# Two transformer blocks on one core: weight products in halves, with attention steps between them

## The chip, the core and the metric

One core of a Trainium2 chip. A core has engines that each run their own instruction stream in order: TensorE (PE, matrix products; its weight load is PEld), VectorE (DVE), ScalarE (ACT), GpSimd (POOL) and SyncE (SP, which here starts the loads). They meet only through semaphores. PSUM has eight banks of 128 x 512 fp32, in which PE leaves its sums. The metric is the device time of one execution in microseconds.

## The reference

256 tokens of width 1024 go through two blocks, all in fp32. Cut to what matters here:

```python
# first block (h: 256 x 1024)
p  = rmsnorm(h) @ w_in               # q, k, v of three branches, 3 x 1024 gates
o_a = stick_breaking(q_a, k_a, v_a)  # 4 heads of 64
o_b = softmax attention over the 64 keys that an index score picks (top-k)
o_c = gates_c[0]*compressed + gates_c[1]*selected + gates_c[2]*window attention
      # compressed keys: gelu(blocks(15 x 2048) @ w1(2048 x 128)) @ w2
merged = sum_j sigmoid(g_j) * (o_j @ w_up[j])        # j = a, b, c; w_up[j]: 256 x 1024
h += merged @ w_out
h += softmax((rmsnorm(h) @ w_q) @ k_mem.T) @ v_mem @ w_o   # 4 heads, 256 memory rows
h += (silu(a) * b) @ w_ffn_out;  a, b = rmsnorm(h) @ w_ffn_in
x = rmsnorm(h)
# second block; shift, scale, gate = (silu(c) @ w_ada + b_ada) in six parts
y = rms(x) * (1 + scale_m) + shift_m
proj = y @ w_in_2                     # fox q, k, v, gate (8 heads), ret q, k, v, gate (4 heads)
x += gate_m * (concat(rms(fox) * ..., rms(retention) * ...) @ w_out_2)
x += gate_f * (relu(y2 @ w_mlp_in)**2 @ w_mlp_out);  y2 = rms(x) * (1 + scale_f) + shift_f
```

## The kernel before

**Weight blocks.** Every large product is made of weight blocks of 1 MB. SP loads a block into a ring of four (`raw`), ACT rounds it to fp32r (`hi`, L1330), DVE subtracts to get the remainder (`lo`, L1649, the *residue*), into rings of three. PE multiplies three times, hi·hi, hi·lo and lo·hi: 48 matmuls of 256 columns for each block. A block's steps are called "round", "residue", "block" and "evac"; `split(s)` enters the first two for all blocks up to s.

**One table of steps.** `plan()` writes a single list. Each engine walks it and issues its part of each step, in the table's order (`run`), so the table sets the order of four in-order queues at once. An engine that waits in one step holds up all that it has later in the table. PSUM banks are leased in table order by `claim`: weight products use the banks "stream" (0, 1), scores "score" (4, 5), transposes "turn" (6, 7), attention sums those of `O_BANK`, `up`, `out` and the like 0 to 3. `claim` waits until the bank's last reader on DVE or ACT is done.

**The first mixer.** Blocks proj 0 to 8 make the projections, gate 0 to 11 the gates, up 0 to 2 the up-projections, out 0 to 3 the output product. Between whole blocks stand the attention's short steps: turn_qk (transposes), stick, suffix, pv_stick (branch a), index and topk (branch b's choice), cmp_hidden, cmp_kv, cmp_scores, turn_cmp_p, cmp_pv (branch c's compression), and for the twelve units of b and c scores, turn_p (transpose of the probabilities) and pv. `units` runs these as a pipeline of pairs, with one gate block after each stage. After gate 11 come turn_o 0, 1, 2 (transposes of the three branch results into `u_hi`/`u_lo`), then up 0, 1, 2, each with its merge: DVE multiplies by gates, POOL adds the second product (L1599), and DVE adds the third. The sums stay in `work`.

**The memory attention.** mem_k, mem_q, mem_v, four units of scores (12 to 15), turn_p, pv, turn_o 3, mem_o. For the scores DVE finds the maximum in PSUM (L2005), scales it (L2007), and in the same step waits for ACT's exponentials of that unit before it frees the bank.

**The second block.** `shifted(n)` interleaves the first product's eight raw parts with the statistics of the row; proj2 0 to 16, out2 2, 3, 0, 1; retention (turn_ret, ret_scores, ret_pv), fox (fox_square, fox_norm, forget, forget_sum, turn_fox, units 16 to 23, mix, mix2, turn_mixed), and "ada" steps on DVE, each one L2146 and seven L2148 for one piece of w_ada.

**Warm-up matmuls.** `IDLE` is a table from a bank's claim to a number of matmuls of ones that `stay_warm` (L733) issues there.

Of the kernel before, what the change touches and what calls it, by code (L numbers as in the profile page):

```python
# [106 lines left out]
def plan():

    blocks = [("proj", j) for j in range(9)] + [("gate", j) for j in range(12)]
    blocks += [("up", j) for j in range(3)] + [("out", j) for j in range(4)]  # L110
# [145 lines left out]
    add("suffix", 0), add("suffix", 1)  # L256
    add("rope1", 0)
    block("proj", 7)
    add("pv_stick", 0), add("pv_stick", 1)
    add("stick", 2), add("stick", 3)  # L260
    block("proj", 8)
    add("turn_qk", 4)
    add("suffix", 2), add("suffix", 3)
    add("gates_c")
    add("rope1", 2)
    block("gate", 0)
    add("turn_qk", 5), add("turn_qk", 6)
    add("pv_stick", 2), add("pv_stick", 3)
    add("o_group", 0)
    add("index", 0), add("index", 1)  # L270
    add("turn_cmp", 0), add("turn_cmp", 1)
# [2093 lines left out]
```

How the kernel before makes its waits and increments, by code:

```python
        def raw_ready(eng, what):  # L652
            i = raw_at[what]
            eng.wait_ge(raw_loaded[i % RAW], 16 * (i // RAW + (i % RAW > 1)))
            return raw[:, i % RAW, :]
# [6 lines left out]
        def wait_filled(eng, key):  # L662
            b, n, _ = lease[key]
            eng.wait_ge(filled[b], n)
            return banks[b]
# [1 line left out]
        def free(ins, key):  # L667
            return ins.then_inc(freed[lease[key][0]], 1)
# [1 line left out]
        def wait_evacuated(eng, key):  # L670
            b, _, n = lease[key]
            eng.wait_ge(freed[b], n)
# [4 lines left out]
        def wait_used(eng, s):  # L677
            at = used_at[s]
            if at[0] == "block_used":
                eng.wait_ge(sem("block_used"), at[1])
            else:
                wait_filled(eng, at[0])
# [32 lines left out]
        @block.tensor  # L715
# [1 line left out]
            def claim(key, bank):  # L717
                if bank in POOL:
                    turn_of[bank] ^= 1
                    bank = POOL[bank][turn_of[bank]]
                if uses[bank]:
                    pe.wait_ge(freed[bank], uses[bank])
                uses[bank] += 1
                lease[key] = (bank, fills[bank] + 1, uses[bank])
                stay_warm(banks[bank], IDLE.get(key, 0))
                return banks[bank]
# [10 lines left out]
                ins.then_inc(filled[b], 1)  # L738
            apart = [0]
            def rows_apart(ins):
                apart[0] += 1
                ins.then_inc(sem("rows_apart"), 1)
                pe.wait_ge(sem("rows_apart"), apart[0])
            pe.wait_ge(sem("ones_set"), 1)
            def product(out, terms):
```

## Time and profile before

| | us |
|---|---|
| median of 3 runs | 874.36 |
| lowest, highest | 868.68, 874.62 |
| profiled execution | 873.8 |
| its span | 871.8 |
| mean granted TensorE clock over the span | 0.947 of full |
| PE, DVE, ACT, POOL busy | 830.4, 626.7, 377.5, 27.4 |

The span is the time from the first to the last instruction that the profile holds; 2.0 us lie around it. Places in the program are given as microseconds from the span's start: the first mixer's projections end near 66, its gates and attention near 201, up near 226.5, out near 248, the memory attention near 291, the feed-forward part near 493; the second block's first product runs to 515, proj2 with retention and fox to 651, out2 to 677, the mlp to the end. "Busy" counts an instruction from start to end also when the clock is low, so a slow stretch shows as a busy PE with a small PEclk.

### The profile page before, as it was taken

Reading aid. Unit: us, or ns where it says so; the run is one execution under the profiler, and the core shown is the slowest. Engines: PE = TensorE matmul, PEld = TensorE weight load, DVE = VectorE, ACT = ScalarE, POOL = GpSimd, SP = SyncE. Lnnn points to the kernel's source line nnn. Section 1 sums busy time; section 2 is a strip of 40 time slices with the busy share of each in tenths; the row PEclk is TensorE's granted clock in tenths of the full one; section 3 lists DMA queues with packets and bytes.
Section 4 is the critical chain, followed back from the end, with each engine's and each line's share of the span. In section 5 each row is a group of like instructions: output and inputs, shape, how many; then the busy total and the mean of one; then the engine's idle time right before and its main releaser. Section 6 shows DMA issues by size and latency. Waiting matters only on the chain.

```text
span 871.8 us, 15595 instructions
## 1 busy us (share of the span) xinstructions
PE 830.4 (95%) x6608; PEld 813.1 (93%) x6608; DVE 626.7 (72%) x978; ACT 377.5 (43%) x503; POOL 27.4 (3%) x27
## 2 busy tenths in 40 slices
PE   8998999998998999999999999979879999999998
PEld 8998987998997989999999999979879999999998
DVE  5867557756886557999998778864676778855553
ACT  6565133553565334232434643334643643333331
POOL 0000000000200000000000000300001000000000
PEclk9997688999998899999999989989979899999999
DMA  9843332132544147788876524543324257765521
GB/s 342 311 176 106 131 111 97 63 132 97 217 156 160 53 143 284 284 298 286 297 277 256 194 97 175 186 173 118 125 97 146 97 193 257 264 226 176 189 97 49
DMA packets 23971, 155.59 MB, mean 178 GB/s; under 512 B 3552, under 2 KB 3680, under 8 KB 5856
## 3 DMA queue, kind: packets, MB, share of 16 engines
q1 hardware_dynamic: 23904, 154.61, 49.2%
q8 instruction: 52, 0.85, 0.4%
q14 instruction: 15, 0.12, 0.0%
HBM read 153.55 MB, written 1.05 MB: 177 GB/s over the span
## 4 chain that ended last, share of the span: by engine, by line
PE 68%; DVE 14%; issue 9%; ACT 6%; POOL 1%; DMA 1%; SPq 0%; DVEq 0%; POOLq 0%; ACTq 0%
PE bank L754 12%; PE bank L756 12%; PE bank L755 12%; PE bank L819 6%; PE bank L822 6%; PE bank L821 6%; DVE sb_lo L1649 4%; ACT sb_hi L1330 4%; PE bank L762 2%; PE bank L764 2%; PE bank L765 2%; PE bank L1083 1%; DMA sb_raw<-in_stream 1%; PE bank L1193 1%; ACT sb_prob L1503 1%
## 5 line engine op out<-in xcount | busy, mean ns | idle before, releaser
L1649 DVE TENSOR_TENSOR sb_lo<-sb_raw,sb_hi 128x2048 fp32r<-128x2048 f32 (+1 forms) x116 | 261.5, 2259 | 119.8 <-ACT sb_hi L1330 118.2
L1330 ACT CAST sb_hi<-sb_raw 128x2048 fp32r<-128x2048 f32 (+1 forms) x116 | 217.4, 1880 | 110.0 <-PE bank L756 58.7
L754 PE MATMUL bank<-sb_u_hi,sb_hi 128*128 128x256 f32 x808 | 234.1, 290 | 0.0
L756 PE MATMUL bank<-sb_u_hi,sb_lo 128*128 128x256 f32 x808 | 231.6, 287 | 0.0
L755 PE MATMUL bank<-sb_u_lo,sb_hi 128*128 128x256 f32 x808 | 231.2, 286 | 0.0
L754 PEld LDWEIGHTS bank<-sb_u_hi,sb_hi 128*128 128x128 f32 x808 | 156.2, 193 | 3.9 <-issue 3.4
L755 PEld LDWEIGHTS bank<-sb_u_lo,sb_hi 128*128 128x128 f32 x808 | 156.6, 194 | 0.3
L756 PEld LDWEIGHTS bank<-sb_u_hi,sb_lo 128*128 128x128 f32 x808 | 156.4, 194 | 0.2
L819 PE MATMUL bank<-sb_hid_hi,sb_hi 128*128 128x256 f32 x432 | 121.4, 281 | 2.4 <-DVE sb_hid_lo L1703 2.4
L822 PE MATMUL bank<-sb_hid_hi,sb_lo 128*128 128x256 f32 x432 | 120.8, 280 | 0.0
L821 PE MATMUL bank<-sb_hid_lo,sb_hi 128*128 128x256 f32 x432 | 120.5, 279 | 0.0
L754 PE MATMUL bank<-sb_hi,sb_u_hi 128*128 128x256 f32 (+1 forms) x336 | 97.5, 290 | 0.0
L756 PE MATMUL bank<-sb_hi,sb_u_lo 128*128 128x256 f32 (+1 forms) x336 | 95.8, 285 | 0.0
L755 PE MATMUL bank<-sb_lo,sb_u_hi 128*128 128x256 f32 (+1 forms) x336 | 95.7, 285 | 0.0
L2148 DVE SCALAR_TENSOR_TENSOR sb_ada_acc<-sb_raw,sb_c_act,sb_ada_acc 128x256 f32<-128x256 f32 x168 | 81.5, 485 | 6.0
L819 PEld LDWEIGHTS bank<-sb_hid_hi,sb_hi 128*128 128x128 f32 x432 | 81.2, 188 | 2.8 <-DVE sb_hid_lo L1703 2.8
L821 PEld LDWEIGHTS bank<-sb_hid_lo,sb_hi 128*128 128x128 f32 x432 | 81.2, 188 | 0.0
L822 PEld LDWEIGHTS bank<-sb_hid_hi,sb_lo 128*128 128x128 f32 x432 | 81.2, 188 | 0.0
L754 PEld LDWEIGHTS bank<-sb_hi,sb_u_hi 128*128 128x128 f32 x336 | 64.7, 192 | 0.3
L755 PEld LDWEIGHTS bank<-sb_lo,sb_u_hi 128*128 128x128 f32 x336 | 64.7, 193 | 0.1
L756 PEld LDWEIGHTS bank<-sb_hi,sb_u_lo 128*128 128x128 f32 x336 | 64.7, 192 | 0.0
L1354 ACT ACTIVATE sb_act_out<-sb_masked 128x256 f32<-128x256 f32 x22 | 9.2, 418 | 102.2 <-DVE sb_masked L1714 102.2
(336 smaller groups left out, 1260.9 us busy)
## 6 DMA issues: line engine op xcount, KB each, us to landing
sb_raw<-in_stream SPq DMA_DIRECT2D x140, 1024.0 KB, 5.0
sb_raw<-in_stream SPq DMA_DIRECT2D x4, 256.0 KB, 6.0
sb_raw<-in_stream SPq DMA_DIRECT2D x2, 512.0 KB, 8.9
sb_mem_t<-in_mem SPq DMA_DIRECT2D x1, 1024.0 KB, 4.8
out<-sb_h SPq DMA_DIRECT2D x4, 256.0 KB, 2.1
...
```

The lines of the kernel that those rows point to most:

```text
L754: nc.tensor.matmul(out, a_hi, b_hi, start=(i == 0), stop=False)
L755: nc.tensor.matmul(out, a_hi, b_lo, start=False, stop=False)
L756: last = nc.tensor.matmul(out, a_lo, b_hi, start=False, stop=(i == n - 1))
L762: nc.tensor.matmul(out, a_hi, b_hi, start=(k == 0 and i in opens), stop=False, skip_group_check=True)
L764: nc.tensor.matmul(out, a_hi, b_lo, start=False, stop=False, skip_group_check=True)
L765: last = nc.tensor.matmul(out, a_lo, b_hi, start=False, stop=(k == KD - 1), skip_group_check=True)
L819: nc.tensor.matmul(out, w_hi[:, k, f], x1, start=(first and k == m == 0), stop=False, skip_group_check=True)
L821: nc.tensor.matmul(out, w_hi[:, k, f], x2, start=False, stop=False, skip_group_check=True)
L822: last = nc.tensor.matmul(out, w_lo[:, k, f], x1, start=False, stop=last_one and k == 1, skip_group_check=True)
L1330: nc.scalar.copy(hi[:, s % SPLIT, 0:n], x[:, 0:n]).then_inc(sem("hi_ready"), 1)
L1649: tt(lo[:, s % SPLIT, 0:n], x[:, 0:n], f32(hi[:, s % SPLIT, 0:n]), ALU.subtract) \
L2148: ins = stt(acc, x[:, k, :], c_act[:, k:k + 1], acc, ALU.mult, ALU.add)
```

## The change

Of the plan, six edits:

1. `half` and an argument `cut` let proj, gate, mem_q and up blocks be issued in two halves with steps between; out2 blocks could before. The short steps of the first mixer are dealt out: some between halves, some between blocks. The two compression products, 32 matmuls of 16 columns in one place, become four parts of 8. cmp_kv moves from ahead of gate 3 to ahead of gate 6.
2. turn_o 0 goes between the halves of gate 5, into tiles of its own (`turned_hi`, `turned_lo`). The up-projections run in the order 0, 2, 1; up 0 waits for branch a alone, pv 2 and 3 stand between its halves, turn_o 2 behind it, turn_o 1 between the halves of up 2. The merged sums move from `work` to slots 4 to 11 of `qk_t`.
3. mem_q in halves, with the row statistics and mem_o's split between; DVE no longer waits for the exponentials of a memory unit, and four nops in o_group 5 free the banks.
4. `shifted`: the sums of squares in four pieces at k = 2 to 5 rather than at k = 2, the statistics behind them.
5. `IDLE` loses up 0, out 0, turn_ret 2 and forget_sum, and keeps the first block and mem_o.
6. Second block: the ada step at j = 9 goes to j = 11; fox's pv steps stand between halves of proj2 14, 15, 16 and out2 2; its scores come one place earlier, ahead of mix and mix2; turn_mixed 2, 3 between the halves of proj2 16.

```diff
+UP_ORDER = (0, 2, 1)
...
+    def steps(some):
+
+        for step in some:
+            if step[0] == "split":
+                split(where[step[1:]])
+            else:
+                if step[0] == "cmp_product" and step[2] == 0:
+                    raw.append(("cmp_w1", step[1]))
+                add(*step)
+                if step[0] == "pv" and step[1] in UNIT_ENDS:
+                    add("o_group", UNIT_ENDS[step[1]])
...
     def shifted(n, s):
 
         for k in range(KD):
-            if k == 2:
+            if 2 <= k < 6:
+                add("ssq_cols", n, k - 2)
+            if k == 5:
                 split(s + 2)
-                rstd(n)
-            if k == 5:
+                add("rstd", n)
+                add("diag", n)
+            if k == 7:
                 add("rstd_row", n)
             add("raw", n, k)
...
-    block("gate", 1)
-    raw.append(("cmp_w1", 0))
-    add("cmp_hidden", 0)
-    raw.append(("cmp_w1", 1))
-    add("cmp_hidden", 1)
-    add("turn_qk", 2), add("turn_qk", 3)
-    add("topk", 0, 0)
-    block("gate", 2)
-    add("cmp_kv")
-    add("topk", 0, 1)
-    block("gate", 3)
-    add("cmp_scores")
...
-    units([(4, 5), (6, 7), (8, 9), (10, 11), (0, 1), (2, 3)], filler)
-    for c in range(3):
-        add("turn_o", c)
-    for j in range(3):
-        block("up", j, ahead=j == 0)
-        add("merge", j)
-        if j == 1:
-            split(where["out", 0])
+    steps([("suffix", 0), ("rope1", 0)])
+    block("proj", 7, between=[("suffix", 1)])
...
+    block("gate", 2, between=[("index", 0), ("turn_qk", 6)])
+    steps([("cmp_product", 0, 0)])
+    block("gate", 3, between=[("cmp_product", 0, 1), ("cmp_hidden", 0)])
+    steps([("cmp_product", 1, 0), ("topk", 0, 0)])
+    block("gate", 4, between=[("cmp_product", 1, 1), ("cmp_hidden", 1)])
+    steps([("index", 1), ("topk", 0, 1)])
+    block("gate", 5, between=[("turn_qk", 2), ("turn_qk", 3), ("turn_o", 0)])
+    steps([("scores", 4), ("scores", 5), ("cmp_kv",)])
+    block("gate", 6, between=[("cmp_scores",)])
+    steps([("turn_p", 4), ("turn_p", 5), ("scores", 6), ("scores", 7), ("topk", 1, 0)])
+    block("gate", 7, between=[("pv", 4), ("pv", 5), ("turn_cmp_p",)])
...
+    block("gate", 11, between=[("pv", 0), ("pv", 1)])
+    steps([("turn_p", 2), ("turn_p", 3)])
+    block("up", 0, between=[("pv", 2), ("pv", 3)])
+    for c in range(4):
+        add("merge", 0, c)
+    add("turn_o", 2)
+    block("up", 2, ahead=False, between=[("turn_o", 1)])
+    add("merge", 1, 0), add("merge", 1, 1)
+    split(where["out", 0])
+    add("merge", 1, 2), add("merge", 1, 3)
+    block("up", 1, ahead=False)
...
-    block("mem_q")
-    rstd(2)
-    split(where["mem_o",])
+    block("mem_q", ahead=False, between=[("ssq_cols", 2), ("rstd", 2), ("split", "mem_o")])
...
-        if j in (4, 6, 9, 12):
+        if j in (4, 6, 11, 12):
             more_ada()
...
+    steps([("scores", 16), ("scores", 17)])
+    block("proj2", 13)
+    steps([("turn_p", 16), ("turn_p", 17), ("scores", 18), ("scores", 19)])
+    block("proj2", 14, between=[("pv", 16), ("pv", 17)])
+    steps([("turn_p", 18), ("turn_p", 19), ("scores", 20), ("scores", 21), ("mix", 0, 0)])
+    block("proj2", 15, between=[("pv", 18), ("pv", 19)])
+    steps([("turn_p", 20), ("turn_p", 21), ("scores", 22), ("scores", 23), ("mix2", 0, 0), ("mix2", 0, 1)])
+    block("proj2", 16, ahead=False, between=[("pv", 20), ("pv", 21), ("turn_mixed", 2), ("turn_mixed", 3)])
+    steps([("turn_p", 22), ("turn_p", 23), ("split", "out2", 3), ("mix", 1, 0)])
+    block("out2", 2, between=[("pv", 22), ("pv", 23), ("mix", 1, 1)])
+    add("mix2", 1, 0), add("mix2", 1, 1)
...
-IDLE = {("block", 0): 16, ("up", 0, 0): 5, ("out", 0): 6, ("mem_o", 0): 5,
-        ("turn_ret", 2): 8, ("forget_sum",): 9}
-O_BANK = {0: 2, 1: 3, 3: 2, 4: 3, 2: 2, 5: 3, 6: 2, 7: 3, 8: 2, 9: 3}
+IDLE = {("block", 0): 16, ("mem_o", 0): 5}
+O_BANK = {0: 2, 1: 2, 3: 3, 4: 2, 2: 3, 5: 3, 6: 2, 7: 3, 8: 2, 9: 3}
...
+            def half(n, cut):
+
+                return range(n) if cut is None else range(n // 2 * cut, n // 2 * (cut + 1))
...
                 for c in half(4, cut):
                     ps = claim(("up", j, c), c)
-                    for i in range(3 if j == c == 0 else 0):
-                        wait_evacuated(pe, ("turn_o", i))
+                    if c == 0:
+                        wait_evacuated(pe, ("turn_o", j))
...
-                    dve.wait_ge(sem("exp_done"), q + 1)
-                    free(nc.vector.engine_nop(), key)
                     return
```

On PE, between gate blocks 1 and 2. In the kernel before, L756 is a gate's last matmul, L1083 both compression products (32 matmuls of 16 columns; the trace has two records for each), L1011 and L1014 transposes of turn_qk:

```order
L755 MATMUL bank<-sb_u_lo,sb_hi 128x256
L756 MATMUL bank<-sb_u_hi,sb_lo 128x256
L1083 MATMUL bank<-sb_cmp_in,sb_raw 128x16 x32
L1011 MATMUL bank<-sb_const,sb_proj 128x128 x4
L1014 MATMUL bank<-sb_const,sb_proj 64x128 x4
L754 MATMUL bank<-sb_u_hi,sb_hi 128x256
L755 MATMUL bank<-sb_u_lo,sb_hi 128x256
```

With the change (L733 to L735 are the former L754 to L756, L1070 the former L1083):

```order
L735 MATMUL bank<-sb_u_hi,sb_lo 128x256
L1070 MATMUL bank<-sb_cmp_in,sb_raw 128x16 x8
L733 MATMUL bank<-sb_u_hi,sb_hi 128x256
...
L735 MATMUL bank<-sb_u_hi,sb_lo 128x256
L1070 MATMUL bank<-sb_cmp_in,sb_raw 128x16 x8
L733 MATMUL bank<-sb_u_hi,sb_hi 128x256
...
L735 MATMUL bank<-sb_u_hi,sb_lo 128x256
L1070 MATMUL bank<-sb_cmp_in,sb_raw 128x16 x8
L733 MATMUL bank<-sb_u_hi,sb_hi 128x256
```

The narrow matmuls stand in groups of 8, with half a gate block (24 matmuls) between two groups.

On DVE, around cmp_kv, before (L1649 residue, L1660 a gate's evacuation, L1953 to L1957 cmp_kv's inputs, L1919/L1920 topk):

```order
L1649 TENSOR_TENSOR sb_lo<-sb_raw,sb_hi 128x2048
L1660 TENSOR_TENSOR sb_gates<-bank,sb_rstd_bc 128x512
L1953 MEMSET sb_hid_v 128x128
L1955 SCALAR_TENSOR_TENSOR sb_hid_t<-sb_hid_t,sb_hid_x 128x2x15
L1956 TENSOR_SCALAR sb_hid_k<-sb_hid_t 128x15
L1957 TENSOR_SCALAR sb_hid_v<-sb_hid_t 128x4x15
L1919 MAX sb_best<-sb_sel_neg 128x8
L1920 MATCH_REPLACE sb_sel_neg<-sb_best,sb_sel_neg 128x128
...
L1923 TENSOR_SCALAR sb_sel_neg<-sb_sel_neg 128x128
```

With the change (L1907/L1908 topk, L1810 turn_o 0, L1637 residue, L1648 a gate's evacuation, L2002/L2005 the scores of units 4 and 5, L1941 to L1945 cmp_kv's inputs):

```order
L1907 MAX sb_best<-sb_sel_neg 128x8
L1908 MATCH_REPLACE sb_sel_neg<-sb_best,sb_sel_neg 128x128
...
L1810 TENSOR_TENSOR sb_turned_lo<-bank,sb_turned_hi 128x512
L1637 TENSOR_TENSOR sb_lo<-sb_raw,sb_hi 128x2048
L1648 TENSOR_TENSOR sb_gates<-bank,sb_rstd_bc 128x512
L2002 SCALAR_TENSOR_TENSOR sb_masked<-bank,sb_const 128x256
L2005 TENSOR_REDUCE sb_neg_max<-sb_masked 128x2
...
L1941 MEMSET sb_hid_v 128x128
L1943 SCALAR_TENSOR_TENSOR sb_hid_t<-sb_hid_t,sb_hid_x 128x2x15
L1944 TENSOR_SCALAR sb_hid_k<-sb_hid_t 128x15
L1945 TENSOR_SCALAR sb_hid_v<-sb_hid_t 128x4x15
```

cmp_kv's inputs came behind one evacuation; now topk (0, 1), a transposed branch's subtraction, a residue, a gate's evacuation and two units of scores are ahead of them.

On DVE, fox, before (L1649 residue; L2264 to L2272 mix2; L2016/L2019 scores; L1822 turn_mixed):

```order
L1649 TENSOR_TENSOR sb_lo<-sb_raw,sb_hi 128x2048
L2264 TENSOR_TENSOR sb_proj<-sb_proj,sb_fstat 128x512
...
L2272 TENSOR_TENSOR sb_proj<-sb_proj 128x512
L2025 RECIPROCAL sb_rden<-sb_den 128x8
L2076 TENSOR_TENSOR sb_work<-bank,sb_rden 128x512
L2016 SCALAR_TENSOR_TENSOR sb_masked<-bank,sb_const 128x512
L2019 TENSOR_REDUCE sb_neg_max<-sb_masked 128x2
...
L1822 TENSOR_TENSOR sb_mixed<-bank,sb_mixed 128x512 x2
L1649 TENSOR_TENSOR sb_lo<-sb_raw,sb_hi 128x2048
```

With the change (L2011/L2064 the end of a group of units, L1637 residue, L2002/L2005 scores 22 and 23, L2249 to L2257 mix2, L1810 turn_mixed):

```order
L2011 RECIPROCAL sb_rden<-sb_den 128x8
L2064 TENSOR_TENSOR sb_work<-bank,sb_rden 128x512
L1637 TENSOR_TENSOR sb_lo<-sb_raw,sb_hi 128x2048
L2002 SCALAR_TENSOR_TENSOR sb_masked<-bank,sb_const 128x512
L2005 TENSOR_REDUCE sb_neg_max<-sb_masked 128x2
...
L2249 TENSOR_TENSOR sb_proj<-sb_proj,sb_fstat 128x512
L2251 SCALAR_TENSOR_TENSOR sb_proj<-sb_proj,sb_gains 128x512
...
L2257 TENSOR_TENSOR sb_proj<-sb_proj 128x512
L1810 TENSOR_TENSOR sb_mixed<-bank,sb_mixed 128x512 x2
L1637 TENSOR_TENSOR sb_lo<-sb_raw,sb_hi 128x2048
```

Scores 22 and 23 and the end of the group stood between mix2 and turn_mixed; they are now ahead of mix2, and turn_mixed follows it at once.

## Rows read from the trace of the kernel before

**Rows 1.** The page: busy time of each engine, then TensorE's granted clock by slices.

```profile
PE 830.4 (95%) x6608; PEld 813.1 (93%) x6608; DVE 626.7 (72%) x978; ACT 377.5 (43%) x503; POOL 27.4 (3%) x27
...
PEclk9997688999998899999999989989979899999999
```

**Rows 2.** The view of windows; the first row names its columns.

```profile
core 0: us, PE busy (x) PEld busy (x) DVE busy (x) ACT busy (x) POOL busy (x), PEclk, DMA share, GB/s
66.00:73.00 7.00, 7.00 (x36) 7.00 (x36) 4.35 (x5) 5.82 (x10) 0.00 (x0) 0.52 0.15 34
66.00:226.50 160.50, 152.03 (x1072) 143.83 (x1072) 105.24 (x210) 62.58 (x113) 7.17 (x4) 0.85 0.29 102
90.00:96.70 6.70, 6.70 (x61) 6.70 (x59) 5.83 (x17) 0.63 (x1) 0.00 (x0) 1.00 0.09 15
96.70:110.40 13.70, 13.70 (x67) 13.55 (x67) 4.37 (x22) 3.84 (x7) 0.00 (x0) 0.50 0.63 224
278.00:291.00 13.00, 10.64 (x50) 10.25 (x49) 5.35 (x8) 3.07 (x4) 0.00 (x0) 0.50 0.46 163
500.20:506.30 6.10, 6.10 (x29) 6.10 (x30) 2.88 (x4) 0.00 (x0) 1.36 (x2) 0.50 0.47 153
592.00:598.00 6.00, 5.12 (x42) 4.04 (x42) 1.29 (x2) 4.31 (x9) 0.00 (x0) 1.00 0.03 12
630.00:637.00 7.00, 0.07 (x1) 0.10 (x2) 6.76 (x11) 0.35 (x1) 0.00 (x0) 0.68 0.40 150
637.00:643.00 6.00, 6.00 (x30) 6.00 (x31) 4.30 (x7) 3.80 (x11) 0.00 (x0) 0.52 0.01 3
```

**Rows 3.** Groups of PE instructions from 90 to 202 us: busy us, mean ns.

```profile
L1083 PE MATMUL bank<-sb_cmp_in,sb_raw 128*128 128x16 f32 x64 | 11.4, 333 | 0.0
```

**Rows 4.** The view of waits, PE: line, releaser, us in total, times, longest.

```profile
PE bank L1291 <- DVE sb_proj L2272: 7.3, 1, 7.3
PE bank L1234 <- DVE sb_soft L2211: 4.6, 1, 4.6
...
PE bank L1090 <- DVE sb_hid_v L1957: 1.5, 1, 1.5
```

**Rows 5.** Groups of DVE instructions, same stretch: busy us, mean ns.

```profile
L1649 DVE TENSOR_TENSOR sb_lo<-sb_raw,sb_hi 128x2048 fp32r<-128x2048 f32 x11 | 25.2, 2293 | 23.9 <-ACT sb_hi L1330 23.8
L1660 DVE TENSOR_TENSOR sb_gates<-bank,sb_rstd_bc 128x512 f32<-128x512 f32 x10 | 6.9, 686 | 4.9 <-PE bank L756 4.9
L2019 DVE TENSOR_REDUCE sb_neg_max<-sb_masked 128x2 f32<-128x512 f32 x6 | 4.1, 686 | 0.2
L1919 DVE MAX8 sb_best<-sb_sel_neg 128x8 f32<-128x256 f32 x8 | 3.4, 427 | 0.2
L1920 DVE MATCH_REPLACE8 sb_sel_neg<-sb_best,sb_sel_neg 128x256 f32<-128x256 f32 x8 | 3.3, 408 | 0.0
...
L2019 DVE TENSOR_REDUCE sb_neg_max<-sb_masked 128x2 f32<-128x256 f32 x6 | 2.5, 420 | 0.2
L1919 DVE MAX8 sb_best<-sb_sel_neg 128x8 f32<-128x128 f32 x8 | 2.3, 293 | 0.2
L1920 DVE MATCH_REPLACE8 sb_sel_neg<-sb_best,sb_sel_neg 128x128 f32<-128x128 f32 x8 | 2.2, 276 | 0.0
```

**Rows 6.** The chain from 266 to 291 us: start us, length us, what.

```profile
271.89 0.69 DVE sb_neg_max L2005
...
274.12 0.68 DVE sb_neg_max L2005
...
276.82 1.41 PE bank L1170 x8
...
279.51 7.08 PE bank L1193 x32
```

**Rows 7.** The chain from 536 to 545 us, same columns.

```profile
540.81 1.78 PE bank L733 x16
```

**Rows 8.** The page's costliest groups: busy us, mean ns of one.

```profile
L2148 DVE SCALAR_TENSOR_TENSOR sb_ada_acc<-sb_raw,sb_c_act,sb_ada_acc 128x256 f32<-128x256 f32 x168 | 81.5, 485 | 6.0
```

More of the change, by code:

```diff
@@ L109, in plan @@
     blocks = [("proj", j) for j in range(9)] + [("gate", j) for j in range(12)]
-    blocks += [("up", j) for j in range(3)] + [("out", j) for j in range(4)]
+    blocks += [("up", j) for j in UP_ORDER] + [("out", j) for j in range(4)]
     blocks += [("mem_k",), ("mem_q",), ("mem_v",), ("mem_o",), ("ffn_in", 0), ("ffn_in", 1)]
@@ L148, in block @@
             add("block", s, 0)
-            for step in between:
-                add(*step)
+            steps(between)
             add("block", s, 1)
@@ L255, in plan @@
     block("proj", 6)
[L256 to L271, printed above, removed]
@@ new lines, in plan @@
+    block("gate", 0, between=[("suffix", 2)])
+    steps([("suffix", 3), ("turn_qk", 5), ("rope1", 3)])
+    block("gate", 1, between=[("pv_stick", 2), ("turn_cmp", 0)])
+    steps([("pv_stick", 3), ("o_group", 0), ("turn_cmp", 1)])
+    block("gate", 2, between=[("index", 0), ("turn_qk", 6)])
[3 more added lines that the diff above has]
+    block("gate", 4, between=[("cmp_product", 1, 1), ("cmp_hidden", 1)])
@@ new lines, in plan @@
+    steps([("index", 1), ("topk", 0, 1)])
[4 more added lines that the diff above has]
+    block("gate", 7, between=[("pv", 4), ("pv", 5), ("turn_cmp_p",)])
+    steps([("turn_p", 6), ("turn_p", 7), ("scores", 8), ("scores", 9)])
+    block("gate", 8, between=[("cmp_pv",), ("o_group", 1)])
@@ new lines, in plan @@
+    steps([("pv", 6), ("pv", 7), ("turn_p", 8), ("turn_p", 9), ("scores", 10), ("scores", 11), ("topk", 1, 1)])
+    block("gate", 9, between=[("pv", 8), ("pv", 9)])
+    steps([("turn_p", 10), ("turn_p", 11), ("scores", 0), ("scores", 1)])
+    block("gate", 10, between=[("pv", 10), ("pv", 11)])
+    steps([("turn_p", 0), ("turn_p", 1), ("scores", 2), ("scores", 3)])
+    block("gate", 11, between=[("pv", 0), ("pv", 1)])
+    steps([("turn_p", 2), ("turn_p", 3)])
+    block("up", 0, between=[("pv", 2), ("pv", 3)])
@@ L305, in plan @@
+    for c in range(4):
[6 more added lines that the diff above has]
+    block("up", 1, ahead=False)
+    for c in range(4):
+        add("merge", 2, c)
     block("out", 0)
@@ L383, in plan @@
             add(*step)
-        if j in (4, 6, 9, 12):
+        if j in (4, 6, 11, 12):
             more_ada()
-    rest = iter(range(13, 17))
-    late = iter([[], [("mix", 0, 0)], [("mix2", 0, 0), ("mix2", 0, 1)], [("mix", 1, 0)], [("mix2", 1, 0)]])
-    early = iter([[], [], [], [("turn_mixed", 2), ("turn_mixed", 3)]])
-    def more():
-        for steps in early:
-            for step in steps:
-                add(*step)
-            break
-        for j in rest:
-            block("proj2", j)
-            break
-        for steps in late:
-            for step in steps:
-                add(*step)
-            break
-    units([(16, 17), (18, 19), (20, 21), (22, 23)], more)
-    add("mix", 1, 1)
-    block("out2", 2)
-    add("mix2", 1, 1)
+    steps([("scores", 16), ("scores", 17)])
[9 more added lines that the diff above has]
+    add("mix2", 1, 0), add("mix2", 1, 1)
     block("out2", 3, between=[("turn_mixed", 0), ("turn_mixed", 1)])
@@ L784, in by_token @@
                     return last
-                for t in range(NT):
+                for t in half(NT, cut):
                     tok = slice(t * P, t * P + P)
@@ L801, in by_feature @@
                     return last
-                for m in range(2):
+                for m in half(2, cut):
                     f = slice(m * P, m * P + P)
@@ L810, in accumulate @@
                 w_hi, w_lo = weights(s)
-                for c in range(4) if cut is None else (2 * cut, 2 * cut + 1):
+                for c in half(4, cut):
                     key = (group, c)
@@ L2060, in o_group @@
                 elif g in (2, 5):
+                    for u in range(12, 16) if g == 5 else ():
+                        free(nc.vector.engine_nop(), ("scores", u))
                     r = inverse_den(0 if g == 2 else 12, 4)
```

162 lines of the change are left out of this document (72 added, 90 removed).

## Prediction, written before the changed kernel had run

> **What bounds the kernel now.** I read the page first. PE is busy for 830.4 of 871.8 us, DVE for 626.7 [rows 1], so PE's queue sets the end and only some 41 us of it are stops. The row of granted clock below it is not flat: digits of 6 to 8 in the slices of the first mixer, near the memory attention, and at four places of the second block; 9 throughout the feed-forward part. A PE that is busy at half clock does half the work, so the second quantity to gain from is the clock. At the mean of 0.947 over the span, 0.053 x 871.8 = 46 us are lost to it, more than to stops.
>
> The view of windows tells where. From 66 to 226.5 us the mean clock is 0.85: 0.15 x 160.5 = 24.1 us of clock, and 160.5 - 152.0 = 8.5 us of stops [rows 2]. In two of its windows PE was busy all the time, 7.00 of 7.00 and 13.70 of 13.70, at 0.52 and 0.50, which is the lower level (1.2 of 2.4 GHz). What PE did before the second fall, from 90 to 96.7, is 6.70 of 6.70 busy at 1.00: no stop, but index and transpose steps of narrow matmuls, and then 64 records of 16 columns, 11.4 us at a mean of 333 ns [rows 2, 3], which with half a gate block fill the slow window. The falls elsewhere follow the memory softmax, the first product of proj2 with its statistics, and the stop of 630 to 637 [rows 2]; none lies in the feed-forward part, where weight blocks follow each other [rows 1]. In this trace, then, the clock goes down after a stretch in which PE does little wide work, stopped or not.
>
> Beside it the Trainium skill, "TensorE: Matmul & The Clock Gate", section "Why this matters for your kernels", wants no idle gaps between matmul bursts; by this alone neither the fall at 66 nor that at 96.7 should be there, since no stop precedes either, so the trace goes beyond that sentence. Part 4 of that page has transposes not count as activity; the window of 592 to 598, almost all transposes of fox, held 1.00 [rows 2], so a short run of them does not lower the clock here.
>
> The view of waits has three stops of note: 7.3 us for mix2's last product before turn_mixed, 4.6 for forget_sum, 1.5 for cmp_kv's inputs [rows 4].
>
> **A: the first mixer, 66 to 226.5.** Nothing is computed less; the order changes. The work at full clock is 160.5 - 24.1 - 8.5 = 128 us. To it come the stops of the new order, from PE's steps against DVE's.
>
> - cmp_kv. DVE has ahead of it topk (0, 1), which ends about with gate 5 (index 1 and topk are about as long on DVE as the block on PE), then turn_o 0's subtraction (0.69, taken as a gate's evacuation), a residue (2.29), an evacuation (0.69), two units' mask and maximum (4 x 0.42) and cmp_kv's own short ones (about 0.7): 6.1 us, while PE has only two units' score products, some 0.4 us [rows 5]. A stop of 5.7 us for 1.5 before. Its lower end is 3 us, if the residue is done earlier.
> - turn_cmp_p, behind topk (1, 0): 4 x (0.43 + 0.41) + 0.4 = 3.8 on DVE and two units of scores, against half a gate on PE: about 2.6.
> - Before up 2, turn_o 2's subtraction stands behind four merges (4 x 0.69) and a residue (2.29), 5 us against the last quarter of up 0: about 3.5.
> - pv_stick 3, 1.2; and 2 us for stops that I can't name, since DVE's 105.2 us of work, 0.66 of the stretch today [rows 2], would be 0.72 of 146.
>
> Together 15 us. Of the clock 3 us stay lost: proj 8 is narrow and unchanged ahead of the fall at 66 (7 us at half is 3.5), and the stops of cmp_kv and up 2 may bring one each. 128 + 15 + 3 = 146: **-14.5 us**. That up 0 no longer stands behind branches b and c adds no gain of its own in this sum: it is why I count no stop before up 0. Ends: -5 (the clock saves only half) and -26 (few stops).
>
> **B: memory attention.** A unit takes 2.23 us, from maximum to maximum (271.89, 274.12), because DVE waits for the exponentials of the unit; its own part is 0.69 + 0.24, ACT's about 1.1 [rows 6]. Three periods less some 1.1 each: 3.1 us earlier for turn_p. pv then took 7.08 us for 32 records at 0.50 clock [rows 2, 6]; if the shorter lull leaves the clock up it is half, 3.5. That is 6.6; the five warm-ups of mem_o remain. The exponentials may now be the bound, so **-6**, ends -2 (only half of the wait) and -8.
>
> **C: shifted.** The window of 500.2 to 506.3 is busy all along at 0.50 [rows 2], 3 us of clock. With the statistics at k = 5 instead of k = 2 the normalised rows come later, and the second block waits for them: I take **-0.8**, ends -3 and +2. The same edit before the mlp: 0.
>
> **D: warm-ups.** Those before turn_ret 2 lay on the chain, 1.78 us [rows 7]; the others filled stops that are there without them: **-1.8**. If the clock falls for want of them it costs some 2 to 3 us at a place: end +3.
>
> **E: ada.** forget_sum waited 4.6 us [rows 4] behind DVE, which had eight ada operations of 0.49, or 3.9 us [rows 8], ahead of it. They go to j = 11, where turn_fox and ret_pv give DVE room: **-3.9**, ends -4.6 and 0 (the wait passes to L1246 or to proj2 12).
>
> **F: fox.** Before, from 630 to 637 PE was busy for 0.07 of 7 us with DVE busy for 6.76, and for the next 6 us PE ran at 0.52: 7.3 of stop and 3 of clock [rows 2, 4]. With the change scores 22 and 23 stand ahead of mix2 on DVE and delay it by 4 x 0.69 = 2.8 us [rows 5], and a gap of much the same length is cut in two, with pv 20, 21 and half a block in it. DVE's sum to the end of turn_mixed is unchanged, and DVE is what bounds here: **-1.5**, ends -5 and +4 (two clock falls for one).
>
> **Sum.** -14.5 - 6 - 0.8 - 1.8 - 3.9 - 1.5 = -28.5 on the profiled execution's 873.8 is 845.3. The median of the runs, 874.36, is 0.6 higher, so 846.
>
> **The rivals.**
>
> *R1: the clock isn't given back.* The short work draws the clock down wherever it stands; in halves of 24 matmuls it does so as well. For it: the falls that have no stop before them. Against: solid weight work holds 1.00, and half a block is 2.8 us of it. Then A keeps its 24.1 of lost clock, with 15 of stops in place of 8.5: 160.5 - 8.5 + 15 = 167, +6.5; B -3, C 0, D -1.8, E -3.9, F +1: 873. The skill's rule on idle gaps speaks for this one: if stops alone lower the clock, dealing out short work gains nothing there, and the new stops cost. Chance 0.1.
>
> *R2: DVE's queue becomes the bound, and the kernel slower.* Every step between two halves needs something of DVE or ACT, and DVE has a residue of 2.29 us [rows 5] ahead of it that the table put there. There are about 20 such places from proj 7 to up 2. In my walk about five of them bite. If each waits for a residue on average, it is 20 x 2.3 = 46 us of stops instead of 15, and with those the clock stays low as before, 12 of its 24.1: A is 128 + 46 + 12 = 186, +25.5, and the rest -10: 890. It decides from the point where stops and lost clock of A pass 32.6 + 14 = 47 us. For it: DVE at 0.72, in steps that can't be put off. Against: DVE keeps two blocks ahead in its residues, and before had idle time behind ACT (23.9 us on the residue's line [rows 5]). Chance 0.06.
>
> *R3: all of it.* DVE is ahead at cmp_kv and up 2, 5 us of stops and 1 of clock: A is 134, -26.5; with the others 834. Chance 0.14.
>
> *R4: A as forecast, the second block against it.* The fox stop is doubled at low clock (+4), ada's wait moves (0), the missing warm-ups cost 3, shifted +2: with A -14.5 and B -6, 862. Chance 0.12.
>
> *Forecast* 0.58, its own range 838 to 855.
>
> **Range and chances.** 832 to 864 leaves out R1, R2 and some tails, under 2 in 10. One per cent, 8.7 us, is about what a measurement of this kernel can tell from no change. Faster by over that (under 865.6): forecast 0.57, R3 0.14, R4 0.08, R1 0.02, in all 0.81. Slower by over it (over 883): R2 0.05 and R1 0.01, 0.06. Within: 0.13.
>
> **What would show it.** A: PEclk of 0.95 or more from the first gate to out 0, and out 0 some 14 us earlier; L1077 (cmp_kv) waiting 4 to 6 us for DVE's L1945; up 0 starting before 185. B: mem's pv in under 4 us. D: no L733 before turn_ret 2. E: forget_sum's wait below 1 us. F: two stops of about 5 us near turn_mixed 2 and pv 22. A clock at half in the same stretches would prove the reading of the clock wrong; stops of over 25 us in A would prove my walk through DVE's queue wrong.

## The result: 1.3% faster, less than half of what was forecast

| | median us | lowest, highest | runs |
|---|---|---|---|
| before | 872.12 | 868.68, 874.62 | 4 |
| changed | 860.31 | 855.70, 863.58 | 4 |

The ratio is 0.987, 95% interval 0.984 to 0.990. Forecast were 846 and a range of 832 to 864: the time lies in the range, but the gain is 12 us where 28 were forecast. The profiled executions stand near the slow end of both kernels, 873.8 and 863.58, 10.2 us apart; two more executions, profiled later, took 871.89 (before) and 864.54 (changed).

The changed kernel's page, PE's line and the row of granted clock, which answer to [rows 1]:

```profile
PE 813.8 (94%) x6552; PEld 797.9 (93%) x6552; DVE 626.4 (73%) x977; ACT 377.6 (44%) x503; POOL 29.6 (3%) x27
...
PEclk9997997899999999999999999989999899999999
```

Its mean clock is 0.962, after 0.947. PE is busy 16.6 us less, and the stops have grown from 41.4 to 47.8 us. The view of waits shows where they are:

```profile
PE bank L1078 <- DVE sb_hid_v L1945: 6.8, 1, 6.8
PE bank L1103 <- DVE sb_cmp_in L1975: 4.1, 1, 4.1
PE bank L1279 <- DVE sb_proj L2257: 3.9, 1, 3.9
PE bank L1279 <- DVE sb_work L2253: 3.6, 1, 3.6
PE bank L1222 <- DVE sb_soft L2196: 3.2, 1, 3.2
PE bank L733 <- DVE sb_u_lo L1810: 3.2, 1, 3.2
```

L1078 is cmp_kv (1.5 us in [rows 4]), L1103 turn_cmp_p, L1279 turn_mixed (once 7.3, now 3.9 and 3.6), L1222 forget_sum (4.6 before), L733 under L1810 the first sum of up 2.

The windows of the changed kernel, with the columns of [rows 2]:

```profile
59.00:225.75 166.75, 149.20 (x1111) 141.66 (x1110) 108.42 (x214) 68.98 (x122) 7.08 (x4) 0.90 0.31 105
66.00:225.75 159.75, 142.20 (x1068) 135.21 (x1068) 105.37 (x211) 64.89 (x116) 7.08 (x4) 0.90 0.31 107
96.50:112.20 15.70, 15.70 (x139) 15.70 (x138) 9.03 (x21) 3.28 (x4) 0.00 (x0) 1.00 0.57 186
124.60:131.40 6.80, 0.00 (x0) 0.00 (x0) 6.49 (x16) 2.08 (x8) 0.00 (x0) 0.74 0.26 77
128.00:138.20 10.20, 6.78 (x31) 6.56 (x31) 3.23 (x10) 2.58 (x11) 0.00 (x0) 0.50 0.30 104
274.50:278.20 3.70, 3.70 (x34) 3.56 (x32) 1.07 (x1) 2.60 (x3) 0.00 (x0) 1.00 0.73 272
63.10:76.70 13.60, 13.60 (x61) 13.07 (x61) 7.13 (x12) 8.56 (x13) 0.00 (x0) 0.50 0.31 94
490.60:501.20 10.60, 10.55 (x90) 10.29 (x88) 5.42 (x11) 4.32 (x8) 1.36 (x2) 1.00 0.30 106
```

The compression product with its gates (96.5 to 112.2) now runs at 1.00, where [rows 2] had 0.50 from 96.7 to 110.4; the memory's pv (274.5 to 278.2) and proj2's first product too. But proj 8 and what follows (63.1 to 76.7) is slow for 13.6 us instead of 6.8, and PE stands still from 124.6 to 131.4 and then runs at 0.50 until 138.2. The fall to 0.50 came at 127.9, 3.5 us before the end of the stop: of its 10.2 us PE was busy for 6.78.

Landmarks on PE, read off the two timelines, give the sum of the forecast term by term:

| from the last landmark to | before | changed | difference | forecast |
|---|---|---|---|---|
| the second block of out (A) | 234.4 | 233.8 | -0.6 | -14.5 |
| start of ffn (B) | 290.6 | 282.5 | -7.5 | -6 |
| start of the second block's first product | 494.1 | 488.4 | +2.3 | 0 |
| turn_ret 0 (C) | 533.0 | 526.0 | -1.3 | -0.8 |
| turn_ret 2 (D) | 542.4 | 533.6 | -1.8 | -1.8 |
| forget_sum (E) | 578.9 | 566.2 | -3.9 | -3.9 |
| scores 16 ahead of proj2 13 (E's work, moved) | 603.2 | 591.3 | +0.8 | 0 |
| the mlp's first product (F) | 678.0 | 666.0 | 0.0 | -1.5 |
| last matmul | 868.3 | 858.1 | +1.8 | 0 |

One row carries the miss: the first mixer, which the change is mostly about, gave nothing.

### The profile page after: what moved, and what is told of

Read it like the earlier page. It is cut to its first block, busy times and chain, and to the rows that moved or that the text cites. A ratio compares the mean times of both kernels' runs of the same rounds, so it can differ in the third digit from the quotient of the medians.

```text
span 861.6 us, 15490 instructions
## 1 busy us (share of the span) xinstructions
PE 813.8 (94%) x6552; PEld 797.9 (93%) x6552; DVE 626.4 (73%) x977; ACT 377.6 (44%) x503; POOL 29.6 (3%) x27
## 4 chain that ended last, share of the span: by engine, by line
PE 73%; DVE 11%; issue 8%; ACT 5%; POOL 2%; DMA 1%; SPq 0%; POOLq 0%; DVEq 0%; ACTq 0%
PE bank L733 13%; PE bank L735 13%; PE bank L734 13%; PE bank L802 7%; PE bank L805 7%; PE bank L804 7%; ACT sb_hi L1318 3%; DVE sb_lo L1637 3%; PE bank L741 2%; PE bank L743 2%; PE bank L744 2%; DMA sb_raw<-in_stream 1%; PE bank L1205 1%; PE bank L1070 1%; DVE sb_ada_acc L2133 1%
## 5 line engine op out<-in xcount | busy, mean ns | idle before, releaser
L1637 DVE TENSOR_TENSOR sb_lo<-sb_raw,sb_hi 128x2048 fp32r<-128x2048 f32 (+1 forms) x116 | 262.3, 2264 | 110.0 <-ACT sb_hi L1318 109.7
L733 PE MATMUL bank<-sb_u_hi,sb_hi 128*128 128x256 f32 x792 | 229.9, 290 | 3.6 <-DVE sb_u_lo L1810 3.2
L735 PE MATMUL bank<-sb_u_hi,sb_lo 128*128 128x256 f32 x792 | 226.9, 286 | 0.0
L734 PE MATMUL bank<-sb_u_lo,sb_hi 128*128 128x256 f32 x792 | 226.3, 286 | 0.0
L733 PEld LDWEIGHTS bank<-sb_u_hi,sb_hi 128*128 128x128 f32 x792 | 152.5, 193 | 6.9 <-issue 5.9
L735 PEld LDWEIGHTS bank<-sb_u_hi,sb_lo 128*128 128x128 f32 x792 | 153.0, 193 | 0.2
L734 PEld LDWEIGHTS bank<-sb_u_lo,sb_hi 128*128 128x128 f32 x792 | 152.9, 193 | 0.3
L733 PE MATMUL bank<-sb_hi,sb_u_hi 128*128 128x256 f32 (+1 forms) x336 | 98.4, 293 | 0.0
L735 PE MATMUL bank<-sb_hi,sb_u_lo 128*128 128x256 f32 (+1 forms) x336 | 96.1, 286 | 0.0
L733 PEld LDWEIGHTS bank<-sb_hi,sb_u_hi 128*128 128x128 f32 x336 | 65.0, 194 | 0.6 <-issue 0.2
L735 PEld LDWEIGHTS bank<-sb_hi,sb_u_lo 128*128 128x128 f32 x336 | 65.1, 194 | 0.0
```

The costliest lines, as they stand in the source:

```text
L733: nc.tensor.matmul(out, a_hi, b_hi, start=(i == 0), stop=False)
L734: nc.tensor.matmul(out, a_hi, b_lo, start=False, stop=False)
L735: last = nc.tensor.matmul(out, a_lo, b_hi, start=False, stop=(i == n - 1))
L1637: tt(lo[:, s % SPLIT, 0:n], x[:, 0:n], f32(hi[:, s % SPLIT, 0:n]), ALU.subtract) \
```

## The experiments

All times are medians; the changed kernel has 860.3, before 872. The changed kernel's executions scatter from 855.7 to 864.5, so against it a difference of under some 5 us is not clear of the scatter: of those below, only cmp_early's, cmp_first's and best_all's gains and a_alone's loss are. Where the times can't decide, the traces have to. Theory 1 when they began: the new order pays for its clock with stops, each of which is one place in DVE's or ACT's queue and brings a fall of the clock behind it. The main rival: the mixer did gain, and another part lost it again. A third: narrow work draws the clock down wherever it stands.

**The mixer's order taken out, and alone.**

```diff
 # all_but_a: the changed kernel with
-UP_ORDER = (0, 2, 1)
+UP_ORDER = (0, 1, 2)
 # the steps from suffix 0 to up as in before, and
-IDLE = {("block", 0): 16, ("mem_o", 0): 5}
+IDLE = {("block", 0): 16, ("up", 0, 0): 5, ("out", 0): 6, ("mem_o", 0): 5}
```

> The changed kernel with the first mixer put back in the order of before (whole blocks, both compression products in one place, turn_o 0 to 2 ahead of up 0, 1, 2, warm-ups of up 0 and out 0 back); memory attention, shifted, ada and fox as changed. Theory 1 (the new order of the first mixer gives nothing, since its stops and the clock falls behind them eat what it saves): 860 to 862, about as the changed kernel. Theory 2 (the first mixer gained as forecast and something behind it lost the gain again): 872 or more.

Measured: 860.19 (855.86 to 864.68), ratio to before 0.988 (0.983 to 0.993).

```diff
 # a_alone: the changed kernel with the memory attention, shifted, ada and fox as before, and
-IDLE = {("block", 0): 16, ("mem_o", 0): 5}
+IDLE = {("block", 0): 16, ("mem_o", 0): 5, ("turn_ret", 2): 8, ("forget_sum",): 9}
```

> The changed kernel with everything but the first mixer's order undone. Theory 1: 871 to 873, within 0.3% of before; its first mixer has some 17 us of stops and some 30 us at half clock. Theory 2: 855 to 860.

Measured: 875.87 (868.04 to 877.96, 10 runs), ratio to before 1.003 (1.000 to 1.006); its trace has much the same stops as the changed kernel's, 6.8 us at cmp_kv among them, and 47.8 us at half clock up to out 1. Theory 2 falls: all of the 12 us come from the small edits, and the mixer's order alone is worth nothing or costs a little.

**How much of the clock belongs to the program.** With the mixer in the old order, all_but_a's trace had out 1 at 226.7, before's at 234.4. So both kernels were profiled in another execution each, with no edit.

> The kernel before once more, for its trace. The kernel with only the first mixer put back had 27 us at half clock there, before had 48 us in the execution that was profiled, with the same order of PE's steps. If the amount hangs on the execution: some 30 to 50 us at half clock from 59 to 226 us, and places that differ from the first profile. If it is fixed by the program: the same eight stretches.

> The changed kernel once more, for its trace: how far the places of the clock's falls differ between two executions of one program. If they are fixed by the program, the same stretches within 1 us; if they also hang on when the execution starts, some stretches come and go and the first mixer's end moves by some us.

The window from proj 8 to out 1 in before's second profiled execution, and two of its slow stretches:

```profile
59.00:231.00 172.00, 155.14 (x1186) 0.93 0.34 119
```

```profile
81.40:91.40 10.00, 8.85 (x37) 7.35 (x36) 8.26 (x27) 1.85 (x2) 0.00 (x0) 0.50 0.13 54
98.40:108.50 10.10, 10.10 (x49) 9.95 (x49) 3.56 (x19) 2.04 (x5) 0.00 (x0) 0.50 0.62 215
```

(Columns of the first: us, PE busy, clock, DMA share, GB/s.) Three falls there, 24 us, less than the 30 to 50 that I had expected, instead of eight with 47.8; and the stops from 59 to out 1 are 16.9 us instead of 10.5. Out 1 starts at 231.0 instead of 234.4: of some 12 us less lost to the clock (half of 24), PE kept 3.4. 6.4 came back as stops, in which PE waits for DVE and ACT; the rest lies in PE's busy time, and I can't place it. More executions say the same: over 32 of the kernel before, whose mean granted clock ranges from 0.945 to 0.964, the time falls by 0.50 us (95% interval 0.37 to 0.64) for each us less of lost clock (one less the mean clock, times the span). That mean counts falls under a stop too, which cost nothing.

Both executions have the falls near 83 and 97, at the memory softmax and at the fox stop; those of before at 66, 117, 138, 148 and 206 are missing in the second. So the order of the program makes some falls likely at a place, and the execution decides on others. The changed kernel's second one: 44.4 us at half clock up to out 1 (37.6 the first time), the stretches at 63 and 128 nearly the same, the others moved. The ffn's fall at 316 is gone and with it the +2.3 of the table above, which is the execution's. The mlp runs in 190.6 us, not 192.1, as one fall there is 3.4 us long instead of 6.8. But its stops are 3.4 us in both, where both traces of before have 1.0, and of the ten traces with the changed statistics three have 190.6 or 190.5 and seven 192.0 or 192.1, for 190.3 twice in before. So its +1.8 is not the execution's alone. What the 2.4 us of new stops come from stays open: a_alone, with the statistics as before, has them too (3.6), and best_all, with the statistics ahead of the mlp as before, 2.5.

**cmp_kv: DVE's place alone.** DVE's chain in the changed kernel, behind index 1 and topk (start, length, what), rows of the chain of waits:

```profile
125.31 0.30 DVE sb_sel_neg L1912
...
126.24 2.28 DVE sb_lo L1637
128.52 0.60 DVE sb_gates L1648
129.12 0.34 DVE sb_masked L2002
...
131.27 0.11 DVE sb_hid_v L1945
131.42 0.61 PE bank L1078 x2
```

From the end of topk at 125.6 to cmp_kv are 5.8 us, of which the residue is 2.3.

```diff
 # cmp_early ("cmp_act" is DVE's part of cmp_kv; PE's and ACT's stay where they are)
-    steps([("index", 1), ("topk", 0, 1)])
+    steps([("cmp_act",), ("index", 1), ("topk", 0, 1)])
```

> One step of the changed kernel moved on DVE alone: cmp_kv's four short instructions ahead of index 1 and topk (0, 1) instead of behind them, a residue, an evacuation and two units of scores. PE's order is unchanged. Theory 1a (the stop at cmp_kv is a matter of DVE's order, and it pulls the clock down behind it): the wait of 6.8 us and the fall of 10.3 us behind it go, 10 to 12 us less than the changed kernel, 849 to 851. Rival 1b (DVE is the bound of this stretch, the wait moves to the softmax of the compressed branch and to up 2): at most 4 us less, 856 or more.

Measured: 853.10 (851.99 to 854.87), 7.2 less than the changed kernel. The wait at cmp_kv is gone, and another stands two steps on, for ACT:

```profile
PE bank L1092 <- ACT sb_vc L1469: 4.4, 1, 4.4
...
PE bank L1103 <- DVE sb_cmp_in L1975: 2.5, 1, 2.5
```

Between the two expectations: DVE's order was the stop, but ACT's copy of cmp_kv's result stood behind the gate and the exponentials, 4.4 us, and the clock fell towards the end of that (131.0 to 141.3). So both queues:

```diff
 # cmp_first: cmp_early, and
-    block("gate", 5, between=[("turn_qk", 2), ("turn_qk", 3), ("turn_o", 0)])
-    steps([("scores", 4), ("scores", 5), ("cmp_kv",)])
+    block("gate", 5, between=[("turn_qk", 2), ("turn_qk", 3), ("cmp_kv",), ("turn_o", 0)])
+    steps([("scores", 4), ("scores", 5)])
```

> cmp_early, and on PE and ACT too cmp_kv now stands between the halves of gate 5, ahead of turn_o 0, so that ACT's copies of its result no longer stand behind gate 5's evacuation and the exponentials of units 4 and 5 (in cmp_early PE still waited 4.4 us for them). If the place in ACT's queue is what was left of that stop: the wait of 4.4 goes and most of the half clock behind it, 4 to 7 us less than cmp_early, 846 to 849. If DVE is the bound there: 852 or more, with the wait at the next step that needs DVE.

Measured: 853.57 (851.44 to 857.58), no better than cmp_early. The stop is down to 1.6 us, yet the clock fell at 132, 142 and 156, 13.6 us together, and the time didn't move. This expectation failed. The trace shows where a part went: the wait for a residue ahead of out 1 is 2.3 us, where cmp_early has 0.7. Its profiled execution was the slowest of the four, and I can't say from one trace whether the program or the execution put the falls there.

**The stop's clock apart from the stop.**

```diff
 # cmp_warm
+                ps = claim(("cmp_kv",), "turn")
+                stay_warm(ps, 29)
                 pe.wait_ge(sem("cmp_hid_ready"), 1)
                 pe.wait_ge(sem("w2_loaded"), 16 * 3)
-                ps = claim(("cmp_kv",), "turn")
```

> The changed kernel with 29 warm-up matmuls of 128 columns (58 records, about 6.4 us) ahead of cmp_kv's wait; the wait itself stays. It tells the price of the stop from that of the clock. If the stop pulls the clock down: no half clock from 128 to 138, 5 us less, 855. If short work does it, and not the stop: the fall stays, 860.

Measured: 859.01 (858.04 to 862.33), 1.3 less, no more than the runs scatter. Its trace, while DVE was still late:

```profile
124.00:131.00 7.00, 7.00 (x62) 6.54 (x61) 6.72 (x15) 1.49 (x6) 0.00 (x0) 1.00 0.17 35
...
131.80:137.70 5.90, 5.84 (x47) 5.59 (x47) 0.23 (x2) 0.45 (x4) 0.00 (x0) 1.00 0.20 86
```

The half gate that ran at 0.50 ran at 1.00, a fall of 3.4 us came only at 137.7, and out 0 began at 221.8 instead of 225.8. The stop of 6.8 us stands without fillers in six traces: five have the fall of 10.2 us, which begins inside the stop, proj_whole's one of 6.8. That the stop pulls the clock down is shown; that the kernel's time gains by fillers is not.

**Narrow work without a stop.**

```diff
 # cmp_whole
-    steps([("cmp_product", 0, 0)])
-    block("gate", 3, between=[("cmp_product", 0, 1), ("cmp_hidden", 0)])
-    steps([("cmp_product", 1, 0), ("topk", 0, 0)])
-    block("gate", 4, between=[("cmp_product", 1, 1), ("cmp_hidden", 1)])
+    steps([("cmp_product", 0, 0), ("cmp_product", 0, 1), ("cmp_hidden", 0)])
+    steps([("cmp_product", 1, 0), ("cmp_product", 1, 1), ("cmp_hidden", 1), ("topk", 0, 0)])
+    block("gate", 3)
+    block("gate", 4)
```

> The changed kernel with both compression products in one place, between gate 2 and gate 3, instead of in four parts between halves. If narrow work without a stop pulls the clock down: a fall of 7 to 14 us behind it as in before, 3 to 7 us more than the changed kernel, 864 to 867. If only stops do: no fall there, 860.

Measured: 863.21 (860.79 to 866.28, 9 runs), 2.9 more, within the scatter. Its windows:

```profile
94.80:98.80 4.00, 4.00 (x39) 4.00 (x38) 3.04 (x4) 0.63 (x1) 0.00 (x0) 1.00 0.23 33
98.80:109.00 10.20, 10.20 (x50) 10.20 (x50) 4.32 (x22) 2.22 (x3) 0.00 (x0) 0.50 0.79 290
```

PE was busy 4.00 of 4.00 us with narrow matmuls and the clock fell to half for 10.2 us, as in before; in four parts between halves it did not. The other traces agree: all four with the two products in one place (both of before, all_but_a, cmp_whole) have a fall between 96.7 and 98.8, and of the ten with four parts none has one there. The reading of the clock on which A rested was right at this place; what the fall costs the kernel, the times don't tell. Of the Trainium skill, "TensorE: Matmul & The Clock Gate", the section "Why this matters for your kernels" asks for no idle gaps between bursts: the 6.8 us stop with the half clock behind it agrees with that. In cmp_whole the clock fell without an idle gap ahead of it, and there the measurement decides.

**proj 7 and 8.**

```diff
 # proj_whole
-    steps([("suffix", 0), ("rope1", 0)])
-    block("proj", 7, between=[("suffix", 1)])
-    steps([("pv_stick", 0), ("stick", 2)])
-    block("proj", 8, between=[("pv_stick", 1), ("stick", 3)])
+    steps([("suffix", 0), ("suffix", 1), ("rope1", 0)])
+    block("proj", 7)
+    steps([("pv_stick", 0), ("pv_stick", 1), ("stick", 2), ("stick", 3)])
+    block("proj", 8)
```

> The changed kernel with proj 7 and 8 whole again and suffix 0 and 1, pv_stick 0 and 1, stick 2 and 3 together between them, as before. If halves with short steps between keep the clock down there (63 to 77 us at half clock in every profile of that order, 66 to 73 in that of before): the fall is 6.8 us instead of 13.6, 3 us less than the changed kernel. If the fall comes from proj 8's 80 columns alone: no difference.

Measured: 856.42 (855.76 to 856.77), 3.9 less, of the size expected but not clear of the changed kernel's scatter. The trace:

```profile
59.00:66.40 7.40, 7.40 (x68) 7.18 (x67) 3.78 (x5) 5.00 (x10) 0.00 (x0) 1.00 0.45 153
66.40:69.80 3.40, 3.40 (x18) 3.40 (x18) 2.23 (x3) 3.38 (x6) 0.00 (x0) 0.50 0.00 0
69.80:77.00 7.20, 7.20 (x63) 7.20 (x63) 4.49 (x12) 3.23 (x4) 0.00 (x0) 1.00 0.42 148
```

The slow stretch at 63 to 77, 13.6 us, stood in every one of the traces with these blocks in halves but cmp_first's (10.2) and cmp_whole's (10.2); with whole blocks it is 3.4 here, and between nothing and 6.8 in the other four traces that have them. Here dealing out made the clock worse: proj 8's matmuls are 80 columns wide, and in halves it lies among short steps all the way. That this is the reason is how I read it; the traces show only that whole blocks lose less clock.

**up 2.**

```diff
 # turn2_early
-    block("up", 0, between=[("pv", 2), ("pv", 3)])
+    block("up", 0, between=[("pv", 2), ("pv", 3), ("turn_o", 2)])
 ...
-    add("turn_o", 2)
 # up_fix: also
+    block("up", 0, ahead=False, ...)
     for c in range(4):
         add("merge", 0, c)
+    split(where["up", 1])
```

> The changed kernel with turn_o 2 between the halves of up 0 instead of behind its four merges, so that DVE subtracts for it ahead of the merges. Theory (the stop of 3.2 us before up 2 is turn_o 2's place in DVE's queue): the stop goes, and with it one fall of 3.4 us, 3 to 5 us less than the changed kernel, 855 to 857. Rival (a residue or the merges bind up 2 anyway): within 1 us.

Measured: 858.73 (854.71 to 863.19), 1.6 less, within the scatter. The stop shrank from 3.2 to 2.6 and changed its releaser:

```profile
PE bank L732 <- DVE sb_lo L1636: 2.6, 1, 2.6
```

L1636 is a residue. I read it as one that up 2 does not need and that stood ahead of the merge that frees the bank; up_fix puts it behind the merges.

> turn2_early, and up 1's residue split behind the merges of up 0 instead of ahead of them; with turn_o 2 early PE still waited 2.6 us, now for a residue, because the bank that up 2 takes is freed by the first merge, and the residue stood ahead of that on DVE. Theory: the stop before up 2 falls below 0.5 us, and its fall of 3.4 us goes, 4 us less than the changed kernel, 856. Rival (the merges themselves bind): 1.5 us or more of it stay.

Measured: 857.22 (856.02 to 858.11), 3.1 less than the changed kernel, as expected but not clear of its scatter. The stop is gone, and so is the fall behind it; from 200 to 220.5 us the clock is 1.00:

```profile
200.00:220.50 20.50, 17.69 (x149) 17.29 (x149) 16.04 (x22) 6.48 (x7) 7.07 (x4) 1.00 0.18 64
```

**All of them.**

```diff
 # best_all: cmp_first + proj_whole + up_fix, the statistics ahead of the mlp at k = 2, and
-    steps([("turn_p", 4), ..., ("scores", 7), ("topk", 1, 0)])
+    steps([("turn_p", 4), ..., ("scores", 7)])
     block("gate", 7, between=[("pv", 4), ("pv", 5), ("turn_cmp_p",)])
-    steps([("turn_p", 6), ...])
+    steps([("topk", 1, 0), ("turn_p", 6), ...])
```

> The changed kernel with cmp_first, proj_whole and up_fix together, topk (1, 0) behind turn_cmp_p instead of ahead of it (PE waited 2.7 to 4.1 us there), and the statistics ahead of the mlp at their old place. Theory (each stop of the first mixer is a place in a queue and brings its own fall): 3.9 + 7 + 4 + 3 + 1.5 = some 19 us less than the changed kernel, 841 to 846. Rival (DVE is the bound, stops move to the next step that needs it): 850 or more.

Measured: **844.34** (842.59 to 844.94), 16 us or 1.9% less than the changed kernel; ratio to before 0.969 (0.965 to 0.973). Its page and the mixer up to out 0:

```profile
PE 802.6 (95%) x6552; PEld 787.7 (94%) x6552; DVE 625.8 (74%) x977; ACT 377.1 (45%) x503; POOL 29.5 (4%) x27
```

```profile
59.00:206.40 147.40, 138.75 (x1108) 132.03 (x1108) 108.10 (x214) 66.44 (x120) 7.07 (x4) 0.97 0.34 118
```

That is within the 841 to 846 expected. 147.4 us for what took 166.75 in the changed kernel (at 0.90) and 167.5 in before (at 0.86). Since all_but_a, with the mixer in the old order, has 860.2, the mixer's new order with its queues put right is worth 16 us, against nothing without that. "Put right" means both: steps moved in DVE's and ACT's queues, and proj 7 and 8 left whole. The parts measured alone, 6.7 (cmp_first), 3.9 and 3.1, give 13.7 of it. topk (1, 0)'s move has no run of its own: the wait of 4.1 at turn_cmp_p is gone, and one for ACT stands further on:

```profile
PE bank L1192 <- ACT sb_prob_t L1515: 2.7, 1, 2.7
```

The statistics' place has no run of its own; the mlp stretch took 191.6 us with the old place, between the 190.6 and 192.1 of the changed kernel's two profiled executions, so nothing of the 16 can be put down to it.

## Why the prediction was wrong

**The term that failed is A, and in it the clock.** The forecast for 66 us to out 0 was 128 us of work at full clock, 15 of stops, 3 of lost clock. The changed kernel took 159.75 us. Its falls there are 31.2 us long, of which 4.1 lie in the stops of cmp_kv and turn_cmp_p, where a PE that stands still loses nothing. That leaves 27.2 us at half clock under a busy PE, 13.6 us lost.

| 66 to out 0 | forecast | measured |
|---|---|---|
| work at full clock | 128 | 128.6 |
| stops | 15 | 17.6 |
| lost clock | 3 | 13.6 |

The work was right. The stops were nearly right in size, and at three of the places named: 6.8 for 5.7 at cmp_kv, 4.1 for 2.6 at turn_cmp_p, 3.2 for 3.5 at up 2. The 1.2 at pv_stick 3 did not come, and 2.5 ahead of out 0 stood in for the 2 that had no place. The lost clock is 10.6 of the 13.8 us that were missing. The 3 us did not hold even what the prediction put into it: it priced the fall at proj 8 alone at 3.5 and added "the stops of cmp_kv and up 2 may bring one each". There were six falls up to out 1:

- The stop at cmp_kv brought 10.2 us at half clock, of which 6.8 under a busy PE: 3.4 us of clock on top of 6.8 of stop. cmp_warm shows that it was the stop.
- proj 8 was called "narrow and unchanged". Its order was changed, and it stood in 13.6 us at half clock, 10.7 of them behind 66, where whole blocks have 0 to 6.8. proj_whole's trace shows it, with 3.4; its time is 3.9 us less, which the scatter could hide.
- Falls of 3.4 us each came at the ends of the stops at turn_cmp_p and up 2, and one behind the stop ahead of out 0, where the warm-ups had stood. One at 165 came behind cmp_pv's narrow matmuls. Of these only up 2's was tested: in up_fix the stop and the fall are gone together.

**A reading that was wrong.** The prediction took PE's work from 90 to 96.7 for index and transpose steps and then the 64 narrow records. The timeline of before has a whole gate block there, 48 matmuls of 256 columns from 87.2 to 94.2, and only the last 2.5 us before the fall are the narrow records. The conclusion for this place stands by cmp_whole (3.9 us of them before the fall), not by that window.

**The base was one execution's.** The 24.1 us that A had to win were the high end: before's second profiled execution lost about 12 there. And what less clock loss gives is not its own length: of 12 us PE kept 3.4 up to out 1, and over the 32 executions of before about half. Stops and clock are not two sums to be subtracted apart, as the 160.5 - 24.1 - 8.5 did. That the small edits alone give all of the measured 12 us agrees.

**R1, "the clock isn't given back",** was the nearest rival: A at +6.5 for a measured -0.6, but mostly for another cause. It had the short work in halves draw the clock down everywhere; that holds at most for proj 8 and the fall at 165. At the compression product dealing out helped, and four of the six falls came with stops. Its B and C were wrong too. R2 needed 20 waits of a residue each; there were four stops of weight. DVE did not bind the stretch: its 108 us of work fit into 147.4.

**B** was right in mechanism and nearly in size: -7.5 for -6, pv 3.70 us at 1.00 for 7.08 at 0.50. **C**: -1.3 for -0.8. **D** came out at its size, -1.8. **E** did too, -3.9, but not its sign: forget_sum's wait is 3.2 us and not under 1. In before nine warm-up matmuls ran for 2.2 us ahead of the wait of 4.6 and covered its beginning, and they went with the change, so the whole pause went from 6.8 to 3.2. E gave 0.8 back where its ada step went, which I had left at nothing. **F**: 0 for -1.5. The stops there, 7.3 and 1.1 us, became 3.9, 1.1 and 3.6, in sum much the same. The one of 3.6 stands ahead of turn_mixed 0 and 1 and not at pv 22. And the fall of 10.2 us had begun inside the stop, with 5.9 us under a busy PE; the two falls of 3.4 have 6.2, so the clock gave nothing back either. The mlp's +1.8, of which some is the execution's, was put at 0: its stops grew by 2.4 us in every trace of the changed kernel. Of A's signs, out 0 came 0.75 us earlier and not 14, and up 0 started at 197 and not before 185.
